# Two attentions of a fused transformer kernel: units taken in pairs, transposes in one burst and values in one burst

## The reference, cut to what matters

```
s = einsum('bqhgd,bkhd->bhgqk', q, k) * scale        # MLA: plain part + rotated part
p = softmax(s, axis=-1)
o = einsum('bhgqk,bkhd->bqhgd', p, v)
y = (o * silu(g)) @ w_out
```

## Time and profile before

| what | value |
|---|---|
| median of 3 runs | 1818.75 us (1818.13 to 1823.63) |
| the profiled execution | 1820.57 us |
| its span in the trace | 1818.8 us |
| TensorE busy | 1752.5 us, 96% of the span |
| VectorE, ScalarE, GpSimd busy | 748.4, 552.7, 154.1 us |
| `gqa` in the trace | from about 1150 to 1311 us |
| `mla` in the trace | from about 1570 to 1759 us |

### The profile page before, as it was taken

One profiled execution on the slowest core, in us unless ns is written; L12 is line 12 of the kernel. 1 busy time (PEld: TensorE's weight loads), 2 busy tenths in 40 slices (PEclk: granted clock), 3 DMA queues, 4 the chain that ended last, 5 costly groups with the idle time before them and its releaser, 6 DMA issues. The chain is left out here.

```text
span 1818.8 us, 24697 instructions
## 1 busy us (share of the span) xinstructions
PE 1752.5 (96%) x9850; PEld 968.5 (53%) x9850; DVE 748.4 (41%) x1591; ACT 552.7 (30%) x1119; POOL 154.1 (8%) x194
## 2 busy tenths in 40 slices
PE   8999988999999899999899999999999999999998
PEld 4444455465544444555464444577745544566763
DVE  2344577142511121433234225477624337466642
ACT  2111577123101111433224212355312233344420
POOL 0310000001111011110100014000000002000000
PEclk9999999999999999999999999999999999999999
DMA  8664688449999999999970222000110012000001
GB/s 282 228 223 185 97 161 115 165 156 403 417 416 416 415 416 418 418 417 418 403 279 15 93 93 93 1 2 1 55 54 35 23 41 93 24 1 2 1 24 46
DMA packets 94594, 324.86 MB, mean 179 GB/s; under 512 B 12792, under 2 KB 31224, under 8 KB 69392
## 3 DMA queue, kind: packets, MB, share of 16 engines
q1 hardware_dynamic: 80624, 302.55, 45.6%
q10 hardware_dynamic: 8656, 12.32, 2.0%
q0 software_dynamic: 5200, 8.41, 1.3%
HBM read 317.58 MB, written 14.30 MB: 182 GB/s over the span
## 5 line engine op out<-in xcount | busy, mean ns | idle before, releaser
L2224 PE MATMUL tail_ps<-arena 128*128 128x512 f32 x488 | 213.8, 593 | 0.0
L1134 PE MATMUL mix_ps<-arena 128*64 128x256 f32 x1568 | 183.2, 387 | 8.3 <-DMA arena<-in_w 5.6
L1010 PE MATMUL mix_ps<-arena,side 128*128 128x512 f32 x384 | 171.5, 604 | 0.6 <-DMA arena<-in_w_in 0.6
L498 DVE TENSOR_SCALAR_CACHE_REDUCE arena<-tail_ps 128x768 f32<-128x768 f32 x128 | 117.5, 956 | 105.9 <-PE tail_ps L358 65.4
L2224 PEld LDWEIGHTS tail_ps<-arena 128*128 128x128 f32 x488 | 92.0, 191 | 110.9 <-issue 110.5
L1134 PEld LDWEIGHTS mix_ps<-arena 128*64 128x64 f32 x1568 | 110.6, 139 | 71.4 <-issue 14.2
L1146 PE MATMUL mix_ps<-arena 128*64 128x512 f32 x512 | 118.6, 606 | 16.5 <-DMA arena<-in_w 15.7
L1010 PEld LDWEIGHTS mix_ps<-arena,side 128*128 128x128 f32 x384 | 72.8, 193 | 96.8 <-issue 95.0
L2224 PE MATMUL tail_ps<-arena,side 128*128 128x512 f32 (+2 forms) x328 | 123.6, 535 | 0.0
L585 ACT ACTIVATE arena<-arena,tail_small 128x768 f32<-128x768 f32 x128 | 118.0, 926 | 5.6 <-DVE arena L498 5.6
L377 PE MATMUL tail_ps<-first,arena 128*128 128x128 f32 x768 | 97.9, 277 | 0.5 <-ACT arena L585 0.5
(11 more groups left out here) (407 smaller groups left out, 2443.6 us busy)
## 6 DMA issues: line engine op xcount, KB each, us to landing
arena<-in_w SPq DMA_DIRECT2D x81, 2048.0 KB, 16.7
arena<-in_l_w_mod SPq DMA_DIRECT2D x16, 1024.0 KB, 6.2
arena<-in_l_w_in SPq DMA_DIRECT2D x16, 1024.0 KB, 7.2
sixth<-in_w SPq DMA_DIRECT2D x15, 1024.0 KB
sixth<-in_w SPq DMA_DIRECT2D x15, 896.0 KB
arena<-in_w_in SPq DMA_DIRECT2D x12, 1024.0 KB, 9.1
arena<-in_l_w_mod SPq DMA_DIRECT2D x16, 512.0 KB, 6.3
residual<-bias_blocks SPq DMA_DIRECT2D x32, 224.0 KB, 12.6
```

The source lines that it names most:

```text
L498: dve.tensor_scalar(self.rows_of(n, x), self.scores_of(n, x), -1.0, None, ALU.mult, ALU.min, accum_out=nm[:, b, x:x + 1]).then_inc(s["maxe ...
L1010: last = pe.matmul(ps[:, u % 4], oT[:, k, t * P:(t + 1) * P], weights.slot(W_IN[n, k // 4], 4, 512)[:, k % 4], start=(k == 0), stop=(k == ...
L1134: last = pe.matmul(out[h * CAP:(h + 1) * CAP, 0:H2], x, block_of(k, h), start=(k == 0), stop=(k == DK - 1))
L2224: last = pe.matmul(out, lhs(k), rhs(k), start=(k == 0), stop=(k == K - 1))
```

## The change

Both attentions get `pairs=True`, and with it:

- TensorE takes units in pairs. For an even a: scores(a+2), weights(a), weights(a+1), [turn of the next group, all its pieces], [inverses of the group before], scores(a+3), values(a), values(a+1). At the start scores(0) and scores(1) come first.
- `first("output")` of `gqa` stands behind scores(3) in step a = 0. On VectorE, `also[0]` stands at the end of that step, behind highest(3).
- The ring's order follows. ScalarE now empties all three banks of unit a, VectorE all three of unit a+1.
- `pr` has room for three units: the two buffers where they were, and a third in the tensor `sixth`, which stood unused in the last two layers. `nm` grows from 2 to 3.
- The orders of VectorE and ScalarE follow the new order.

```diff
+    def place_pairs(self):
+        self.ring = {}
+        for j in range(len(self.turns[0])):
+            self.place(("turn", 0, j), j % 2)
+        for a in range(0, self.N, 2):
+            for n in (a, a + 1):
+                for j in range(len(self.weight_pieces(n))):
+                    self.place(("weights", n, j), int(n == a))
+            for j in self.turns_behind(a):
+                self.place(("turn", self.units[a][0] + 1, j), j % 2)
+            if a - 1 in self.closes:
+                self.place(("inverse", self.closes[a - 1]), 0)
+        self.place(("inverse", self.ogs - 1), 0)
...
+    def turns_behind(self, a):
+        g = self.units[a][0]
+        return range(len(self.turns[g + 1])) if a == self.first_of[g] and g + 1 < self.groups else range(0)
...
+    def probabilities(self, n):
+        return self.mem["pr"][n % 3] if self.pairs else self.mem["pr"][:, n % self.PRB]
...
+        if self.pairs:                                    # tensor
+            scores(1)
+            for a in range(0, N, 2):
+                if a + 2 < N:
+                    scores(a + 2)
+                weights(a)
+                weights(a + 1)
+                if self.turns_behind(a):
+                    turn(units[a][0] + 1, self.turns_behind(a))
+                if a - 1 in self.closes:
+                    inverses(self.closes[a - 1])
+                if a + 3 < N:
+                    scores(a + 3)
+                if a == 0:
+                    first("output")
+                values(a)
+                values(a + 1)
+            inverses(self.ogs - 1)
+            return
...
+        if self.pairs:                                    # vector
+            highest(1)
+            for a in range(0, N, 2):
+                if a + 2 < N:
+                    highest(a + 2)
+                self.empty_weights(dve, 0, a + 1)
+                self.empty_turn(dve, 0, units[a][0] + 1, self.turns_behind(a))
+                if a - 1 in self.closes:
+                    divide(self.closes[a - 1])
+                if a + 3 < N:
+                    highest(a + 3)
+                if a + 1 in self.closes:
+                    og = self.closes[a + 1]
+                    k = len(self.members[og])
+                    dve.wait_ge(s["exped"], (a + 2) * L)
+                    dve.reciprocal(rc[:, og % 2, 0:k, :], sm[:, og % 2, 0:k, :]).then_inc(s["inverted"], 1)
+                    finish(og)
+                if also is not None and a in also:
+                    also[a]()
+            divide(self.ogs - 1)
+            return
...
+        if self.pairs:                                    # scalar
+            exponential(1)
+            for a in range(0, self.N, 2):
+                self.empty_weights(act, 1, a)
+                if a + 2 < self.N:
+                    exponential(a + 2)
+                self.empty_turn(act, 1, units[a][0] + 1, self.turns_behind(a))
+                if a + 3 < self.N:
+                    exponential(a + 3)
+            return
...
-    nm, sm, rc = little(2, 2), little(2, 4, 2), little(2, 4, 2)
+    nm, sm, rc = little(3, 2), little(2, 4, 2), little(2, 4, 2)
...
+    pr = [view(arena, 27648, 2, AT * P), view(arena, 29184, 2, AT * P), view(sixth, 0, 2, AT * P)]
...
-    gqa = Attention(nc, m, sem_of("gqa_"), dict(S=S, T=T, O=O, pr=view(arena, 27648, 2, 2, AT * P), ...), ..., spread=1, copied=True)
+    gqa = Attention(nc, m, sem_of("gqa_"), dict(S=S, T=T, O=O, pr=pr, ...), ..., copied=True, pairs=True)
-    mla = Attention(nc, m, sem_of("mla_"), dict(S=S, T=T, O=O, pr=view(arena, 27648, 2, 2, AT * P), ...), ..., spread=2, copied=True, ...)
+    mla = Attention(nc, m, sem_of("mla_"), dict(S=S, T=T, O=O, pr=pr, ...), ..., copied=True, pairs=True, ...)
```

More of the change, by code:

```diff
@@ L242, in __init__ @@
     def __init__(self, nc, m, s, mem, units, L, LEAD, turns, heads, score_parts, value_of, dv, out_of=None, gate=False, combine=None,
-                 bias=None, rows_to=None, extra=None, ready=None, spread=None, rotated=None, copied=False):
+                 bias=None, rows_to=None, extra=None, ready=None, spread=None, rotated=None, copied=False, pairs=False):
         self.nc, self.m, self.s, self.mem, self.units, self.L, self.LEAD, self.turns, self.heads = nc, m, s, mem, units, L, LEAD, turns, heads
@@ L252, in __init__ @@
         self.copied = copied or bias is not None
-        self.N, self.groups, self.PRB = len(units), len(turns), LEAD + 1
+        self.N, self.groups, self.PRB, self.pairs = len(units), len(turns), 3 if pairs else LEAD + 1, pairs
         N = self.N
@@ L260, in __init__ @@
         self.turn_step = {}
+        if pairs:
+            self.place_pairs()
+            return
         for g in range(1, self.groups):
@@ L282, in __init__ @@
         self.emptied = [sum(1 for _, a, _ in self.ring.values() if a == act) for act in range(2)]
+    def place_pairs(self):
[11 more added lines that the diff above has]
+        self.place(("inverse", self.ogs - 1), 0)
+        self.by_place = {r: (act, k) for r, act, k in self.ring.values()}
+        self.emptied = [sum(1 for _, a, _ in self.ring.values() if a == act) for act in range(2)]
+    def turns_behind(self, a):
+        g = self.units[a][0]
+        return range(len(self.turns[g + 1])) if a == self.first_of[g] and g + 1 < self.groups else range(0)
     def place(self, key, act):
@@ L308, in rows_of @@
         _, _, lo, hi, _, _ = self.units[n]
-        rows = self.mem["pr"][:, n % self.PRB, x, 0:(hi - lo) * P]
+        rows = self.probabilities(n)[:, x, 0:(hi - lo) * P]
         return rows if self.rotated is None else rows.rearrange("p (c k) -> p c k", c=2)
+    def probabilities(self, n):
+        return self.mem["pr"][n % 3] if self.pairs else self.mem["pr"][:, n % self.PRB]
     def slot(self, n):
@@ L376, in weights @@
                 for z, (x, kt) in enumerate(tiles):
-                    ins = pe.transpose(Tp[:, bank, z * P:(z + 1) * P], pr[:, n % self.PRB, x, kt * P:(kt + 1) * P], m["ident"])
+                    ins = pe.transpose(Tp[:, bank, z * P:(z + 1) * P], self.probabilities(n)[:, x, kt * P:(kt + 1) * P], m["ident"])
                 ins.then_inc(s["turned"], 1)
@@ L583, in exponential @@
                     act.wait_ge(*((s["inverted"], units[n][4] - 1) if self.rows_to is None else (s["o_done"], units[n][4] - 1)))
-                in_, scale = (pr[:, b, x, 0:k], -1.0) if self.copied else (self.scores_of(n, x), 1.0)
-                act.activation(pr[:, b, x, 0:k], in_, ACT.Exp, bias=nm[:, b, x:x + 1], scale=scale,
+                in_, scale = (self.probabilities(n)[:, x, 0:k], -1.0) if self.copied else (self.scores_of(n, x), 1.0)
+                act.activation(self.probabilities(n)[:, x, 0:k], in_, ACT.Exp, bias=nm[:, b, x:x + 1], scale=scale,
                                accum_out=sm[:, og_b, z, x:x + 1]).then_inc(s["exped"], 1)
@@ L593, in scalar @@
             exponential(n)
+        if self.pairs:
[7 more added lines that the diff above has]
+                    exponential(a + 3)
+            return
         for n in range(self.N + 1):
@@ L1969, in context_gates_at, with second_layers @@
     return view(arena, 25600, DK, CTX)
-def second_layers(nc, c, m, A, base, side_w, extra, arena, ring_in, rows_in, mods, tabs_2, l1_tabs):
+def second_layers(nc, c, m, A, base, side_w, extra, arena, sixth, ring_in, rows_in, mods, tabs_2, l1_tabs):
     small = c.enter_context(nc.sbuf_tensor("tail_small", [P, 960], F32))
@@ L2130, in gqa_scores @@
         pe.wait_ge(s["ev_act"], units.by[unit["g", DK - 1]][1] + 1)
-    gqa = Attention(nc, m, sem_of("gqa_"), dict(S=S, T=T, O=O, pr=view(arena, 27648, 2, 2, AT * P), pT=view(arena, 8192, 2, 2 * AT, P), nm=nm, sm=sm, rc=rc, ratio=None,
+    gqa = Attention(nc, m, sem_of("gqa_"), dict(S=S, T=T, O=O, pr=pr, pT=view(arena, 8192, 2, 2 * AT, P), nm=nm, sm=sm, rc=rc, ratio=None,
                                                 wide=view(side_w, 3072, 2, 4, 2, 64)),
@@ L2136, in second_layers @@
                     lambda p, x, kt: proj[:, kt, 256 + (p // 2) * 64:256 + (p // 2 + 1) * 64], 64,
-                    lambda p: gT_x[:, p], gate=True, ready=dict(ring=gqa_ready, scores=gqa_scores, output=gqa_output), spread=1, copied=True)
+                    lambda p: gT_x[:, p], gate=True, ready=dict(ring=gqa_ready, scores=gqa_scores, output=gqa_output), copied=True, pairs=True)
     qn, qr, kn, krT = view(arena, 8192, 2, SEQ), view(arena, 9216, 2, SEQ), view(side_w, 0, 2, AT * P), view(side_w, 1536, AT * P)
@@ L2157, in mla_scores @@
         pe.wait_ge(s["ev_act"], units.by[unit["h", DK - 1]][1] + 1)
-    mla = Attention(nc, m, sem_of("mla_"), dict(S=S, T=T, O=O, pr=view(arena, 27648, 2, 2, AT * P), pT=view(base, at6, 2, 2 * AT, P), nm=nm, sm=sm, rc=rc, ratio=None,
+    mla = Attention(nc, m, sem_of("mla_"), dict(S=S, T=T, O=O, pr=pr, pT=view(base, at6, 2, 2 * AT, P), nm=nm, sm=sm, rc=rc, ratio=None,
                                                 wide=view(side_w, 3072, 2, 4, 2, 64)),
```

(4 more changed lines are left out.)

## The result

| | before | after |
|---|---|---|
| median | 1818.44 us (6 runs, 1813.72 to 1823.63) | 1830.85 us (6 runs, 1829.73 to 1832.66) |
| profiled execution | 1820.57 us, span 1818.8 | 1830.76 us, span 1828.9 |
| mean granted clock of the runs | 0.994 (77 runs over the study) | 0.992 (12 runs) |

The ratio is 1.0068, 95% interval 1.0054 to 1.0083: slower by 12.4 us. A second series of the same kernel gave 1829.06 and 1.0061 (1.0044 to 1.0077). The forecast was 1824, +5, with a range to 1830.

The account below looks back on a forecast made before the run. TensorE, busy 96% of the span, was taken as the bound, so only its own sequence counted. Gains of 15.4 us against losses of 20.4 gave +5.0 on 1818.75, say 1824, with a range of 1816 to 1830.

Parts of the forecast that it names:

- The wait before values(0): At gqa's start, TensorE stands until highest(3) and the two additions are done: +3.3 us.
- Phases saved: In both attentions, each of 32 pairs has one transpose and one value phase fewer, 0.30 a pair: -9.6 us.
- The edge from scores to values: New edge on TensorE in each pair, priced at 0.15 us like other changes of kind, with ends 0 and 0.30.
- The ring inside the burst: Six banks through a ring of three, transposes waiting for ScalarE's copies 0.48 apart: 0.19 us a burst, +6.0 in all.
- The rival of 0.60: ScalarE's copies in the burst start 0.60 us apart: +4 more, +9 in all, 1828 us; chance 0.15.
- the seam: Rival: an overhead between the two units' transposes, up to +4.8 us, 1829; chance 0.10.
- The Trainium skill's figures for ScalarE: For ScalarE's back-to-back copies, an estimate of 0.52 us apart for 512, adding 1.4 us over about 17 bursts.
- The ring behind the burst: Turns and inverses after the burst wait for VectorE's copies, 0.60 apart: +4.2 us in mla, +3.4 in gqa.
- The starts: scores(2), now before weights(0), waits for highest(1) without transposes as cover: +1.5 us in gqa, +2.0 in mla.
- The sum: Over both attentions, gains of 15.4 us against losses of 20.4: net +5.0.
- The rival on the other side: The ring doesn't hold TensorE: -8.6 us, 1810, or with half of it -2, 1817; chance of holding less 0.17.
- parts 1 and 2: The ring inside the burst and the ring behind the burst, in both attentions: 13.6 us lost together.

Follow-up runs that it names:

- e1: The changed kernel with the two additions of the context's output moved on VectorE from behind highest(3) to ahead of highest(1): 1823.98 us.
- e9: e7 with the two additions put back behind highest(3), as in the change: 1821.49 us.
- e7: The rebalanced kernel: both starts, with ScalarE emptying five of six banks and a turn's even pieces, the turn's before exponential(a+2): 1813.96 us.
- e4: The kernel before the change, without pairs, with only also[0] moved one step later on VectorE, behind highest(2) and unit 1's copies: 1824.20 us.
- e2: The changed kernel with weights(0) put ahead of scores(2) on TensorE in both attentions: 1826.72 us.
- both starts: The changed kernel with the edits of e1 and e2 together: 1822.94 us.
- half copies: e1 with every copy of transposed weights cut to its first half in both attentions, the values using old data for the rest: 1813.97 us.

## Why the prediction was wrong

- **The wait before values(0)** ("TensorE stands for +3.3 [...] the other engines have nothing to do then"). This is the step that failed. The wait itself is there, released as forecast, and is 3.26. But the sum prices it at its length alone and puts what the clock does behind it at nothing. In the change's trace the matmuls behind it ran at a granted clock of 0.50 and cost 3.0 more, values lasting 5.39 instead of 2.84, and 1.7 fell behind the wait for highest(1). Removing or adding the wait before values(0) was worth 6.7 (e1), 6.8 (e9 against e7), 5.4 (e4, 3.0 long in the old order) and 3.0 (e2 against both starts). Of these the clock accounts for 3.0, 4.7, 2.7 and 0.2, on average 2.7 with a standard error of 0.7. So a kernel with this wait most likely loses clock, but that the wait is the cause isn't shown: one pair of four shows nothing, and in the traces a stretch at 0.50 followed directly in both of the change and in e2, not in e4 and e9. When and where the clock falls stays open.
- **Phases saved, -9.6.** Right: 0.30 for a pair, shown with the ring's waits out of the way. The edge from scores to values, which no row had shown, costs what the others do.
- **The ring inside the burst, +6.0.** Right: 0.20 a burst against 0.19, and the copies were 0.49 apart, near the end I chose. The rival of 0.60 and the seam are out. With half copies the plain pairs lose exactly this 0.20.
- **The Trainium skill's figures for ScalarE** (ScalarE: Activation LUTs, What ACT_TABLE_LOAD costs) would put the copies 0.52 apart, by the estimate in the prediction; the trace has 0.49.
- **The ring behind the burst, +7.6.** Right by group: `gqa` with three pieces +0.42 (19.83 for two pairs against 19.41), with one piece -0.13, `mla` +0.06, where the terms give +0.34, -0.20 and -0.03. These differences, 0.07 to 0.09 for each group, add up to some 1.1, most of what the forecast missed at full clock.
- **The starts, +3.5.** The waits came as forecast: 1.9 for the maximum in `gqa`, where 0.5 was before, and two of 1.93 in `mla`, where one was. But the reason was half of it. Putting the transposes back under the wait returned next to nothing, because waits of 0.9 and 1.1 for VectorE's copies took its place.
- **The sum.** At full clock the change costs 6.9 and 6.4 in its two series, the forecast was 5.0, so 1.5 to 2 us are small errors of many terms, none over 0.1 a pair. The clock took another 4 (14.3 on average against 10.4). In means over both series that is 10.6 us against the 77 runs of the kernel before; the 12.4 of the first comparison lies between two medians of 6 runs. The small errors and the clock were both needed to leave the range, and only just: the second series, 1829.06, lies inside it. What the prediction named as signs of being wrong, plain pairs of 8.5 or over 8.9 or no wait of 3.3, did not show.
- **The rival on the other side**, a ring that doesn't hold TensorE, was wrong for the kernel as it is: plain bursts lose 0.20 each. The half copies show what the ring holds back in all: 10.0 in means, 12.0 at full clock, where parts 1 and 2 of the forecast had 13.6.

## What to carry to other kernels

Merging phases of one kind on TensorE does save 0.15 us for each edge, but a longer burst is only as fast as the engines that empty its ring: write down when each bank comes free, and give banks to the engine that is idle at that moment, not a unit to an engine. After reordering a steady loop, look at its first step. A one-time job that was tucked in there, like the two additions here, can end up behind work that waits on the very engine that waits for it. And when a change makes TensorE wait in a new place, look at the granted clock behind it before you price the wait at its length: here some 3 us of waiting were worth 3.0 to 6.8.

## What the runs showed of the hardware that was not expected

- All eleven profiled executions have stretches at a granted clock of 0.50, not always at the same places, though TensorE is busy 96% of the span. They took 10 to 17 us of an execution, and they make up most of the spread of a kernel: over 77 runs of the kernel before, the time spreads with a standard deviation of 3.0 and the time at full clock with 1.9. The 12 runs of the change average 14.3 us lost by the clock, those 77 runs 10.4, the rebalanced kernel 8.6, the half copies 13.6.
- Two adjacent units' values cost nothing at their seam, nor do the transposes of two units once their banks are free: 24 transposes in 2.77 us with the edge, in the kernel with half copies.
- ScalarE's copies of PSUM banks followed each other at 0.49 us for 128x512, faster than VectorE's 0.60.
